# Outputs of both branches kept unsplit until sample attention, and cache pages of three batches read beside prompt attention

## What is computed

```python
def ssm_branch(...):
    ...
    y = jax.nn.gelu(y.reshape(B, T, SSM_WIDTH))
    y = y * jax.nn.sigmoid(y @ w_glu.astype(f32))

def prompt_sparse_attention(q, k, v, qi, wi, ki, rel_bias):      # 8 blocks of 128 tokens, 8 heads of 64
    ...
def sample_sparse_attention(layer, q, k_new, v_new, ...):        # 4 pages of 128 tokens a batch, and 4 new tokens
    ...
    k_sel = jnp.where(in_past, cache_k[layer, phys, off], k_new[b_ix, nidx])
    v_sel = jnp.where(in_past, cache_v[layer, phys, off], v_new[b_ix, nidx])

def merge_and_ffn(x, y_ssm, y_attn, g_ssm, g_attn, w_ssm_out, w_attn_out, w_o, norm2_g, w_up, w_down):
    mix = jax.nn.sigmoid(g_ssm) * (y_ssm @ w_ssm_out) + jax.nn.sigmoid(g_attn) * (y_attn @ w_attn_out)
    x = x + mix @ w_o
    h = rms_norm(x, norm2_g)
    return x + jnp.square(jax.nn.relu(h @ w_up)) @ w_down
```

## Time and profile before

| | |
|---|---|
| median of three runs | 2018.72 us |
| the profiled execution's own time | 2016.42 us |
| its span, first to last instruction | 2014.6 us |
| TensorE busy | 1776.4 us (88%) |
| VectorE, ScalarE, GpSimd busy | 998.6, 562.2, 398.6 us |
| granted TensorE clock, mean | 0.952 |

### The profile page before, as it was taken

The page is one execution under the profiler, slowest core; times in us unless marked ns, Lnnn a source line. Parts: engine busy times, 40 slices in busy tenths (PEclk is TensorE's granted clock), DMA queues, the critical chain, the costliest instruction groups (busy, mean ns, idle before and its releaser), DMA issues. The chain is left out here.

```text
span 2014.6 us, 28381 instructions
## 1 busy us (share of the span) xinstructions
PE 1776.4 (88%) x11098; PEld 1572.4 (78%) x11112; DVE 998.6 (50%) x1953; ACT 562.2 (28%) x1069; POOL 398.6 (20%) x213
## 2 busy tenths in 40 slices
PE   2869566999999988885598995999999999999999
PEld 2849335899999955553398995988999999999987
DVE  3845988999995547652143132233333333333334
ACT  4323250222322245441121033222222222222220
POOL 5217100011120000000043134111122111111110
PEclk9979788999999989998699997999999999999999
DMA  5171008353231111006542311111111111111102
GB/s 141 47 119 49 27 16 74 98 161 109 93 99 43 39 50 43 1 1 199 167 152 74 117 56 42 42 42 42 42 42 42 44 56 46 42 42 42 42 21 86
DMA packets 120469, 135.34 MB, mean 67 GB/s; under 512 B 23490, under 2 KB 101282, under 8 KB 120338
## 3 DMA queue, kind: packets, MB, share of 16 engines
q1 hardware_dynamic: 120370, 134.01, 23.5%
HBM read 109.80 MB, written 24.18 MB: 67 GB/s over the span
## 5 line engine op out<-in xcount | busy, mean ns | idle before, releaser
L2510 DVE TENSOR_TENSOR view_at<-psum,view_at 128x512 f32<-128x512 f32 (+1 forms) x288 | 199.3, 692 | 183.0 <-PE psum L141 183.0
L139 PE MATMUL psum<-mix_hi,up_hi 128*128 128x352 f32 x768 | 249.9, 325 | 15.9 <-DVE hid_lo L2501 12.3
L140 PE MATMUL psum<-mix_lo,up_hi 128*128 128x352 f32 x768 | 248.1, 323 | 0.0
L141 PE MATMUL psum<-mix_hi,up_lo 128*128 128x352 f32 x768 | 247.8, 323 | 0.0
L139 PE MATMUL psum<-dn_hi,hid_hi 128*128 128x512 f32 x576 | 227.8, 395 | 0.0
L141 PE MATMUL psum<-dn_hi,hid_lo 128*128 128x512 f32 x576 | 226.8, 394 | 0.0
L140 PE MATMUL psum<-dn_lo,hid_hi 128*128 128x512 f32 x576 | 226.4, 393 | 0.0
L2501 DVE TENSOR_TENSOR hid_lo<-psum,hid_hi 128x352 fp32r<-128x352 f32 x96 | 50.4, 525 | 353.8 <-ACT hid_hi L2467 353.8
L1423 DVE TENSOR_SCALAR_CACHE_REDUCE view_at<-view_at,view_at 128x384 bf16<-128x384 f32 (+6 forms) x231 | 196.0, 912 | 1.2
L139 PE MATMUL psum<-h_hi,w_hi 128*128 128x352 f32 x600 | 195.1, 325 | 0.2 <-issue 0.2
L141 PE MATMUL psum<-h_hi,w_lo 128*128 128x352 f32 x600 | 193.5, 323 | 0.0
(11 more groups left out here) (351 smaller groups left out, 3448.8 us busy)
## 6 DMA issues: line engine op xcount, KB each, us to landing
view_at<-w_in SPq DMA_DIRECT2D x18, 1024.0 KB, 5.4
view_at<-w_up SPq DMA_DIRECT2D x16, 1024.0 KB, 5.6
view_at<-w_down SPq DMA_DIRECT2D x16, 1024.0 KB, 4.9
gate_dram<-view_at SPq DMA_DIRECT2D x48, 176.0 KB, 1.9
view_at<-gate_dram SPq DMA_DIRECT2D x16, 528.0 KB, 4.5
view_at<-cache_k SPq DMA_DIRECT2D x32, 256.0 KB, 3.7
view_at<-cache_v SPq DMA_DIRECT2D x32, 256.0 KB
view_at<-u_dram SPq DMA_DIRECT2D x16, 290.0 KB, 14.9
```

Source lines behind the costliest of these rows:

```text
L139: nc.tensor.matmul(out, lhs[0], rhs[0], start=start, stop=False)
L140: nc.tensor.matmul(out, lhs[0], rhs[1], start=False, stop=False)
L141: return nc.tensor.matmul(out, lhs[1], rhs[0], start=False, stop=stop)
L2510: nc.vector.tensor_tensor(x1[r, i, cols], psum[r, 4 + (2 * par + j) % 4, :], x1[r, i, cols], ALU.add).then_inc(add_done, 1)
```

## The change

Between the GLU and sample attention the outputs of both branches stay single float arrays (`ys_raw`, `ya_raw`); `ys_hi` and `ya_hi` are written only in sample attention, by ScalarE, and `ys_lo` and `ya_lo` by GpSimd, in place of the arrays they come from. The memory of the two missing halves is free until then, and takes pages. There are now places for the keys and values of batches 0 to 5 (batch 6 uses those of batch 0, batch 7 those of batch 3), and each batch has semaphores of its own. The pages of batches 0 to 2 are loaded in the block of prompt attention. The diff, cut to its core:

```diff
-    ysG = (view_r("ys_hi", 2200, 4, T), view_r("ys_lo", 6424, 4, T))
+    ys_raw = view(2200, 4, T)
+    ysG = (view_r("ys_hi", 6424, 4, T), view_r("ys_lo", 2200, 4, T))
...
                 nc.scalar.activation(sgl[:, j % 2, :], psum[:, n % BANKS, 0:TH], ACT.Sigmoid).then_inc(sig_done, 1)
-                act.wait_ge(glu_done, j + 1)
-                nc.scalar.activation(ysG[0][:, m, TH * t3:TH * (t3 + 1)], glu[:, j % 2, :], ACT.Copy).then_inc(hi_done, 1)
...
-                if j >= 2:
-                    dve.wait_ge(lo_done, j - 1)
-                v.tensor_tensor(glu[:, j % 2, :], y2[:, m, cols], sgl[:, j % 2, :], ALU.mult).then_inc(glu_done, 1)
-                dve.wait_ge(hi_done, j + 1)
-                v.tensor_tensor(ysG[1][:, m, cols], glu[:, j % 2, :], f32(ysG[0][:, m, cols]),
-                                ALU.subtract).then_inc(lo_done, 1)
+                v.tensor_tensor(ys_raw[:, m, cols], y2[:, m, cols], sgl[:, j % 2, :], ALU.mult).then_inc(glu_done, 1)
...
-    yaT = (view_r("ya_hi", 10648, 4, T), view_r("ya_lo", 14872, 4, T))
+    ya_raw = view(10648, 4, T)
+    yaT = (view_r("ya_hi", 14872, 4, T), view_r("ya_lo", 10648, 4, T))
...
-    Kp = [view(o, NPG, AW) for o in (19096, 21144, 27544)]
-    Vp = [view(o, NPG, AW) for o in (23192, 25240, 29592, 39832, 41880)]
+    Kp = [view(o, NPG, AW) for o in (19096, 6424, 14872, 21144, 27544, 39832, 19096, 21144)]
+    Vp = [view(o, NPG, AW) for o in (23192, 8472, 16920, 25240, 29592, 41880, 23192, 25240)]
...
         @block.sync                       # prompt attention
-            load_pages(sp, 0)
+            for b in range(2):
+                load_new_v(sp, b)
+            for b in range(3):
+                load_pages(sp, b)
...
         @block.gpsimd
-            pool.wait_ge(pool_done, 9)
-            for i in range(NT - 1):
-                pool.wait_ge(hi_done, i + 1)
-                nc.gpsimd.tensor_tensor(yaT[1][:, :, i * P:(i + 1) * P], inv_T[i % 2], f32(yaT[0][:, :, i * P:(i + 1) * P]),
-                                        ALU.subtract).then_inc(lo_done, 1)
...
                 dve.wait_ge(out_of[0], taken(inv_group[i], 0))
-                v.tensor_tensor(inv_T[i % 2], psum[:, 6 + i % 2, :].rearrange("p (m t) -> p m t", t=P), inv_T[i % 2],
-                                ALU.mult).then_inc(y_done, 1)
+                v.tensor_tensor(ya_raw[:, :, i * P:(i + 1) * P], psum[:, 6 + i % 2, :].rearrange("p (m t) -> p m t", t=P),
+                                inv_T[i % 2], ALU.mult).then_inc(y_done, 1)
...
-                if m == 3 and i:
-                    high(i - 1)
...
-            high(NT - 2)
...
         @block.sync                       # sample attention
-            for b in range(1, BG + 1):
-                if b >= 3:
-                    sp.wait_ge(kT_done, 4 * (b - 2))
-                load_pages(sp, b)
-            sp.wait_ge(kT_done, 4 * (BG - 1))
-            load_keys(sp, BG + 1)
+            load_new_v(sp, 2)
+            load_new_v(sp, 3)
+            load_pages(sp, 3)
+            load_keys(sp, 4)
+            load_keys(sp, 5)
+            sp.wait_ge(kT_done, 4)
+            load_keys(sp, 6)
+            load_new_v(sp, 4)
+            load_values(sp, 4)
+            load_values(sp, 5)
+            sp.wait_ge(kT_done, 16)
+            load_keys(sp, 7)
             sp.wait_ge(pv_done, 1)
-            load_values(sp, BG + 1)
-            for b in range(BG + 2, NB):
-                sp.wait_ge(kT_done, 4 * (b - 2))
-                load_pages(sp, b)
+            for b in range(5, NB):
+                load_new_v(sp, b)
+            for b in range(6, NB):
+                load_values(sp, b)
             load_wb(sp, 0)
...
         @block.scalar
             for b in range(BG + 2, NB):
                 keys(b)
+                for m in range(2 * (b - BG - 2), 2 * (b - BG - 1)):
+                    act.wait_ge(pv_done, 1)
+                    nc.scalar.activation(ysG[0][:, m, :], ys_raw[:, m, :], ACT.Copy).then_inc(high_done, 1)
             high(0)
             exps(1)
-            probs(1)
+            for m in range(4):
+                nc.scalar.activation(yaT[0][:, m, 0:SEQ], ya_raw[:, m, 0:SEQ], ACT.Copy).then_inc(high_done, 1)
+                if m == 1:
+                    probs(1)
             high(1)
+
+        @block.gpsimd
+        def _(pool):
+            for m in range(4):
+                pool.wait_ge(high_done, m + 1)
+                nc.gpsimd.tensor_tensor(ysG[1][:, m, :], ys_raw[:, m, :], f32(ysG[0][:, m, :]),
+                                        ALU.subtract).then_inc(low_done, 1)
+            for m in range(4):
+                pool.wait_ge(high_done, 4 + m + 1)
+                nc.gpsimd.tensor_tensor(yaT[1][:, m, 0:SEQ], ya_raw[:, m, 0:SEQ], f32(yaT[0][:, m, 0:SEQ]),
+                                        ALU.subtract).then_inc(low_done, 1)
```

More of the change, by code:

```diff
@@ L1115, in hybrid_kernel @@
     gst = view(31640, 2, TH)
-    glu = view(31640, 2, TH)
     y2 = view(32344, 4, T)
@@ L1519, in hybrid_kernel @@
     nmax2 = small(2, 2)
-    k_in = [sem(f"k_in{q}") for q in range(3)]
-    v_in = [sem(f"v_in{q}") for q in range(5)]
+    k_in = [sem(f"k_in{q}") for q in range(NB)]
+    v_in = [sem(f"v_in{q}") for q in range(NB)]
     PAIRS = [(i, m) for i in range(NT - 1) for m in range(4)]
@@ L1563, in load_new_v @@
     def load_new_v(sp, b):
-        sp.dma_start(vnew[b % 5][0:NS, :], nv[1][NS * b:NS * (b + 1), :]).then_inc(v_in[b % 5], 16)
+        sp.dma_start(vnew[b % 5][0:NS, :], nv[1][NS * b:NS * (b + 1), :]).then_inc(v_in[b], 16)
     def load_keys(sp, b):
         for j in range(NPG):
-            load_page(sp, Kp[b % 3][:, j, :], "cache_k", page_of(sp, b, j), k_in[b % 3])
+            load_page(sp, Kp[b][:, j, :], "cache_k", page_of(sp, b, j), k_in[b])
     def load_values(sp, b):
-        load_new_v(sp, b)
         for j in range(NPG):
-            load_page(sp, Vp[b % 5][:, j, :], "cache_v", page_of(sp, b, j), v_in[b % 5])
+            load_page(sp, Vp[b][:, j, :], "cache_v", page_of(sp, b, j), v_in[b])
     def load_pages(sp, b):
-        load_new_v(sp, b)
         for j in range(NPG):
             page = page_of(sp, b, j)
-            load_page(sp, Kp[b % 3][:, j, :], "cache_k", page, k_in[b % 3])
-            load_page(sp, Vp[b % 5][:, j, :], "cache_v", page, v_in[b % 5])
+            load_page(sp, Kp[b][:, j, :], "cache_k", page, k_in[b])
+            load_page(sp, Vp[b][:, j, :], "cache_v", page, v_in[b])
     def row_bank(u, hh):
@@ L1873, in hybrid_kernel @@
         lo_done = sem("s7_lo")
+        high_done = sem("s7_high")
+        low_done = sem("s7_low")
         @block.sync
         def _(sp):
[L1877 to L1882 removed]
+            load_new_v(sp, 2)
[10 more added lines that the diff above has]
+            load_keys(sp, 7)
             sp.wait_ge(pv_done, 1)
[L1884 to L1887 removed]
+            for b in range(5, NB):
+                load_new_v(sp, b)
+            for b in range(6, NB):
+                load_values(sp, b)
             load_wb(sp, 0)
@@ L1894, in keys_T @@
             def keys_T(b):
-                pe.wait_ge(k_in[b % 3], 16 * NPG * (b // 3 + 1))
+                pe.wait_ge(k_in[b], 16 * NPG)
                 for m in range(4):
@@ L1900, in keys_T @@
                     for j in range(NPG):
-                        last = tr(psum[:, n % 2, j * P:(j + 1) * P], Kp[b % 3][:, j, m * P:(m + 1) * P], ident)
+                        last = tr(psum[:, n % 2, j * P:(j + 1) * P], Kp[b][:, j, m * P:(m + 1) * P], ident)
                     last.then_inc(kT_done, 1)
@@ L1933, in values @@
                 for b in range(BG):
-                    pe.wait_ge(v_in[(BG * g + b) % 5], 16 * (NPG + 1) * ((BG * g + b) // 5 + 1))
+                    pe.wait_ge(v_in[BG * g + b], 16 * (NPG + 1))
                 for j in range(NPG):
                     for b in range(BG):
-                        mm(psum[HR * b:HR * (b + 1), 7, :], PTb[:, j, HR * b:HR * (b + 1)], Vp[(BG * g + b) % 5][:, j, :],
+                        mm(psum[HR * b:HR * (b + 1), 7, :], PTb[:, j, HR * b:HR * (b + 1)], Vp[BG * g + b][:, j, :],
                            start=(j == 0), stop=False, tile_position=(0, HR * b))
```

9 lines of the change are left out of this document (1 added, 8 removed).

## The result

The changed kernel took 1986.55 us (median of four runs, 1985.83 to 1991.10), the kernel before 2019.27 in the same comparison (four runs, 2017.76 to 2021.01). The ratio is 0.9842, 95% interval 0.9825 to 0.9859: 1.6% faster. The forecast was 1986.0.

A forecast was written before the change was run, and what follows sets the result against it. TensorE, busy 88%, had one reachable hole: 31.7 us waiting in sample attention for key pages from SP's queue. Sample attention -29.7 and two tails gave -32.8: 2016.42 to 1983.6, plus 2.3 for the median, forecast 1986 us, range 1979 to 1993.

The forecast's parts named there:

- Part 1: End of the GLU: the block ends behind the last multiply instead of the last subtraction, 1.08 us less.
- Part 2: End of prompt attention: the block ends behind VectorE's last product instead of GpSimd's subtraction, 2.00 us less.
- Part 3: Prompt attention: sixteen pages loaded beside it cost nothing, bounds 0 and +2 us.
- Part 4: SP's queue in sample attention, counted from its start S: last page of keys 7 issued S + 34.0, landed S + 37.2.
- Part 5: Sample attention: TensorE's work ahead of keys 7 ends at S + 35.8, so it waits about 1.4 us for them.
- Part 6: Sample attention behind keys 7: 22.3 us plus 1.0 for two `ya` copies; stage ends S + 60.5, GpSimd's subtractions just hidden.
- The sum: Whole kernel: sample attention 29.7 us less, with both block ends 32.8 less; forecast 1986 us, chance 0.60.
- Rival A: Prompt and sample attention: TensorE's clock stays up, in values(1), keys 7 and first prompt tiles; 1980.5 us, chance 0.19.
- Rival B: Sample attention: TensorE or SP later than counted, through low-clock values(0), a 4.5 us landing, page-load disturbance; 1989 us, chance 0.11.
- Rival C: End of sample attention: GpSimd's `ya` subtractions, slowed to 4.41 us each beside VectorE, end the stage; +6.3, 1992 us, chance 0.06.
- Rivals D and E: Sample attention: early pages bring nothing, 2015.6 us, chance 0.02; or GpSimd becomes the bound by far, kernel slower, chance 0.01.

The follow-up runs named there:

- second execution: The changed kernel with no edit, profiled once more: 1982.6 us, sample attention 60.2 us.
- first execution: The changed kernel's first profiled execution, the slowest of its four, against the kernel before: 1991.1 us, sample attention 64.0 us.
- the experiment with `ys` later: Changed kernel with ScalarE's four `ys` copies, and so GpSimd's subtractions of `ys`, moved behind keys 7: sample attention 62.9 us.
- the registers alone: Changed kernel with only the 20 page numbers of batches 3 to 7 read into SP's registers during prompt attention: 1982.13 us, ratio 0.9814.

## Why the prediction was right, step by step

- Part 1, the end of the GLU: right. The last multiply ended at 745.76 and prompt attention began at 746.05. The stages ahead of it, which I had left at the durations of before, scattered by 4.8 us between two executions.
- Part 2, the end of prompt attention: right, 163.2 us against 165.2 in both executions.
- Part 3, sixteen pages at no cost: right, from the same two stretches; with the pages of batches 1 and 2 taken out again it was 163.2 as well.
- Part 4, SP's queue: the last page of keys 7 at S + 34.0 in the forecast, 35.0 and 36.5 measured. The step of 1.10 was right: nearly all single pages follow each other at 1.09 to 1.12 us. The 1.0 is made of a start 0.2 us later (keys 4 at S + 8.3 and not 8.1) and of two irregular steps in the second execution, 1.53 us behind the first page of keys 4 and 1.42 among the values of batch 4, which is 0.75 more than two steps. The first execution's further 1.5 is about what the issue held for 2.08 us cost (1.7 more than usual). I had no term for such steps; over five executions with this order the page went out between S + 34.5 and 36.5. The last page of keys 7 landed in 3.0 us in the second execution (3.2 forecast) and 3.7 in the first.
- Part 5, TensorE's arrival: I had batch 3 land at S + 10.3 and be no wait. It was one of 2.9 to 3.1 us in both executions, for two reasons. Keys 0 to 2 ran at the upper level (granted clock 1.00), so TensorE was through with them 8.6 us after the start and not 11.1; and the last page of batch 3 took 4.8 and 5.0 us to land where I had 3.8, and was there at S + 11.5 to 11.7. Behind that wait the clock fell (0.50 for keys 3), and logits(0) took 5.8 to 5.9 us instead of 3.9; keys 6, at 1.00, took 2.6 instead of 3.7. TensorE arrived at keys 7 at S + 37.1 (35.8 forecast) and waited 0.95 us (1.4 forecast) in the second execution. The waits for keys added up to 6.0 and 3.9 us, as forecast near 6 or below, but not "nearly all ahead of batch 7": half or more stood ahead of batch 3.
- Part 6, behind keys 7: 23.3 us in the forecast, 23.8 and 22.1 measured. The stage of before ended at 997.42 and not at 997.2, so the 22.3 it was built on should have been 22.5. The two `ya` copies cost 1.61 - 0.69 = 0.92 of the 1.0 I gave them, and GpSimd's last subtraction ended at S + 59.0 in the second execution (58.8 forecast). The stop for VectorE's held copy, 1.0 to 1.2 us, is missing from the sum. In the second execution it cost nothing net: the transposes of keys 7 ran at the upper level and took 3.7 us with all their stops, as before; values(1) took 5.31 us instead of 6.30. In the first they took 4.5, and logits(1) 4.64 instead of 3.91. So the terms err by up to 1 us each, in both directions.
- The sum: 32.8 us less was forecast, 32.7 measured (2019.27 to 1986.55). The mechanism carries it, but that the two agree so closely is luck. The same kernel gave 1991.1 and 1982.6 us in its two profiled executions, and terms above are off by 1 to 2 us in both directions.
- Rival A (the clock stays up) held in part: keys 0 to 2 and some of values(1) ran at the upper level. Rival B's late queue is what the first profiled execution drew, though not by B's causes: values(0) ran at the upper level (3.64 us), and an issue was held. Of the 8.5 us between its two executions 4.8 lie ahead of prompt attention. Rival C named the right pair of engines and the wrong victim: GpSimd kept its 2.40 us a subtraction, and VectorE's copy was the one held. The trace of the kernel before already had such a case, right behind the row that I had used: while the subtraction that began at 98.18 was still running, VectorE's next instruction, an eighth larger than the 2.29 us one, took 4.64 us.

```profile
100.37 4.64 DVE L501 TENSOR_TENSOR view_at<-view_at,view_at 128x2304 f32<-128x2304 f32 x1
```

- Rivals D and E didn't occur; but the experiment with `ys` later shows that GpSimd bounds the stage at S + 62.6 as soon as its start slips by 5 us.

The sentence of the Trainium skill, "GPSIMD Engine Reference", section "Key points", by which I had called the tail free of contention, names two kinds of VectorE instruction that contend with GpSimd: those with two SBUF inputs and those "in a 2-port perf mode". I had used the first kind alone. The copy that was held has one SBUF input and writes to SBUF, so by that sentence it could only be of the second kind; no run here shows in which mode it ran. The 128x512 evictions beside the same subtractions, which read PSUM, kept their 0.68 us. My reading of the rule was too narrow, and the conclusion that the tail is free of contention was wrong.

## What to carry to other kernels

When one engine's queue feeds a stage, count its whole queue and not only the item that is waited for: moving an item forward only moved the wait to what it had overtaken, while making every item cheaper (page numbers read beforehand, 1.10 us down to 0.5 to 0.6) shortened the stage. Work moved onto GpSimd can cost through a neighbour: look for VectorE's short copies inside SBUF that TensorE waits for. And profile a changed kernel twice before explaining the last few us: the same code differed by 8.5 us in total and by 3.8 us in this stage.

## What the runs showed of the hardware that I had not expected

- A VectorE copy of 128x16 floats within SBUF, 0.17 us alone, took 0.32 to 2.05 us in six executions in which GpSimd was subtracting 128x1056 floats beside it, and ended with the subtraction each time; copies of 128x512 out of PSUM did not slow down (0.68 us).
- About half of SP's 1.10 us for a page goes with the reading of its number: 0.34 to 0.38 us is the DMA instruction, and with the number in a register pages follow each other at 0.51 us (0.60 on average with the irregular steps). The load itself (`TENSOR_LOAD`) is 0.27 us; the rest is what SP does with the number.
- One DMA instruction of SP was held for 2.08 us, and in another run for 1.79, where 0.38 is usual; most of the other runs had one of 0.5 to 1.4 us. What held them is open.
- With pages issued every 0.5 to 0.6 us the median time to landing rose from 3.0 to 6.3 us (6.4 with the registers alone), at a DMA share of 0.93.
- The same matmuls of values(1) took 3.64 to 6.55 us over these runs, at a granted clock of 1.00 to 0.55, behind an idle of 2 to 2.5 us and one of 0.7 to 1.6 us (5.8 in one run). Why one execution falls to the lower level there and the next doesn't is open.
